# A two-layer hybrid diffusion block: merge units of mLSTM and GLA dealt out anew, GLA's scores issued a tile ahead

## The chip, the cores and the metric

The kernel runs on one core of a Trainium2 chip. The metric is the device time of one execution in microseconds. TensorE (PE) does matmuls and transposes, ScalarE (ACT) activations and copies out of PSUM, VectorE (DVE) elementwise work and scans, GpSimd (POOL) masks and indirect DMAs, SyncE (SP) streams the weights. Engines run their own instruction lists and meet at semaphores.

## The reference

Two layers over 256 context and 512 latent tokens, width 1024, float32. Each layer: adaLN-modulated norm, four token-mixer branches of width 256, their merge, and an expert-choice MoE with 16 experts. In layer 1 only the latent tokens are needed as queries. What matters here:

```
mLSTM (4 heads, 2 directions):  s = exp(d_log - m_t) * (q k^T);  h = (s v) / max(|den|, exp(-m_t))
GLA   (4 heads, 2 directions):  S_t = diag(exp(ge)) S + k^T v;   o = mask(q_dec k_inv^T) v + q_dec S0
merge:  g = sigmoid(h @ w_gate + b_gate);  p = y_branch @ w_branch
        y = sum over the four branches of g * p, then @ w_out
```

The merge of one branch needs only that branch's output y and the layer's input h. So the merge of branch n can be computed while branch n+1 is.

## The kernel before

Each engine has its own function per stage: `mla`, `mlstm`, `gla`, `diff`, `merge`, `moe`. The token axis is held as 6 tiles of 128 (2 context, 4 latent). TensorE writes to eight PSUM banks. They are dealt to three kinds of job by `ring`: "a" (ScalarE empties them), "d" (VectorE empties them) and "g" (merge units). A job that would take a bank still in use waits for its semaphore (`a_free`, `d_free`, `g_free`).

A **merge unit** is one 128 x 256 piece of a branch's gate and projection: 8 matmuls over h (line 539) and 2 over y (line 541) on TensorE, each shown as two in the profile since float32 takes two passes; a Tanh on ScalarE (`gates`); one or two operations on VectorE (`merged`). A branch has 24 units in layer 0 and 16 in layer 1. Those of the first branch run inside mLSTM, those of mLSTM inside GLA, and so on. How many run where is written out by hand and must be the same on all three engines: `ML_GAP` at the opening of mLSTM, `ml_quota` in its 24 steps, `ML_END` after them; `gl_quota` and `GL_END` for GLA. Before the change `ML_GAP` and `ML_END` are 3; the steps get 18 units in layer 0 and 10 in layer 1, spread evenly. GLA has 4, 1 and 1 per step (first direction) and 3, 2 and 1 per step (second) in layer 0; 4, 1, 1 per step and 1, 0, 1 per step in layer 1; then 2.

**mLSTM.** TensorE projects (lines 460, 467) and runs the opening units. VectorE scans the gates for two directions on 8 partitions and gives `ml_m`; ScalarE's Exp gives `ml_rows`, on which TensorE transposes (line 673). POOL carries rows through DRAM and back as a broadcast (`ml_bc0`). Then 4 heads of 6 steps: `products` (line 682, q k^T for key tile j), ScalarE's weights W(j) (waits for PV of step j-2, since `m_W` has two buffers), POOL's mask, VectorE's multiply (line 1482, gives `ml_s`), TensorE's PV (line 698). Products run a step ahead. At the end of a head VectorE normalises the sums (`x_free`) before it takes the next head's products.

**GLA.** After the projections and the alpha matmuls (line 729), ScalarE and VectorE form decays. Per direction: VectorE's scan gives `gl_g`, four Exps of ScalarE give `gl_e`, VectorE's operands give `gl_ops`; TensorE transposes (line 474), 11 chunk matmuls (line 741) feed VectorE's state recurrence (lines 1470 and 1482, `gl_state`); then per query tile scores (line 749), VectorE's mask into `g_A` (`gl_att`), and matmuls with the states and values (lines 758, 761). Units in GLA cycle through two banks, 6 and 7.

The weights stream through three ring slots of 2 MB each, in the order of `layer_pieces`.

Of the kernel before, what the change touches and what calls it, by code (L numbers as in the profile page):

```python
# [19 lines left out]
ALU = mybir.AluOpType  # L20
AF = mybir.ActivationFunctionType
AX = mybir.AxisListType
P = 128
# [4 lines left out]
T = CTX + LAT  # L28
NT = T // P
# [130 lines left out]
def hybrid_layers(nc, I, out, stop=None):  # L160
    ctx = ExitStack()
    with ctx:
# [104 lines left out]
        def ml_quota(L):  # L267

            n = branch_units(L) - ML_GAP - ML_END
            return [(s + 1) * n // (4 * NT) - s * n // (4 * NT) for s in range(4 * NT)]  # L270

# [5 lines left out]

        ML_GAP, ML_END, GL_END, DF_GAP, DF_END = 3, 3, 2, 2, 2

        def gl_quota(L):  # L280

            return (4, 1, 1, 3, 2, 1) if len(chunks(L)) == 3 else (4, 1, 1, 1, 0, 1)

# [66 lines left out]
        g_y = area(19 * T, NT * 256).rearrange("p (t c) -> p t c", t=NT)  # L350
        g_A = area(21 * T, 512)
        g_sl = area(21 * T + 512, 256)
# [79 lines left out]
        def _(pe):  # L432
# [218 lines left out]
            def mlstm(L):  # L651
# [33 lines left out]
                for h in range(4):  # L685

                    products(h, 0)
                    for j in range(NT):
                        if j + 1 < NT:
                            products(h, j + 1)  # L690
                        merge_units(L, quota[h * NT + j])
                        pe.wait_ge(sems["ml_s"], c.nth("ml_s"))
                        if j == 0 and h >= 1:
                            pe.wait_ge(sems["x_free"], c.nth("x_free"))
                        for d in range(2):
                            ts = ml_tiles(L, d, j)
                            for t in ts:
                                ins = pe.matmul(banks[6 + d][:, t * 65:t * 65 + 65], m_W[:, j % 2, d, t * P:(t + 1) * P],
                                                m_v[:, j, h, :], start=(j == 0 and t == ts[0]),
                                                stop=(j == ml_last(d, t)), skip_group_check=True)  # L700
                        ins.then_inc(sems["pv_done"], 1)
# [5 lines left out]
            def gla(L):  # L707
# [18 lines left out]
                for d in range(2):  # L726
                    for off, n in SEG:
                        b = job("a")
                        pe.matmul(b[:, 0:n], wa[0:16, d, :], g_a[0:16, d, off:off + n], start=True, stop=True).then_inc(sems["a_done"], 1)
                for d in range(2):  # L730

                    merge_units(L, quota[3 * d])
                    pe.wait_ge(sems["gl_ops"], c.nth("gl_ops"))
# [3 lines left out]
                    for i in range(11):  # L737
                        ch = gla_chunk(d, i)
                        t, r = ch // 2, (ch % 2) * 64
                        b = job("d")  # L740
                        pe.matmul(b[:, 0:256], g_ke[r:r + 64, t * P:(t + 1) * P], g_v[r:r + 64, t, :],
                                       start=True, stop=True).then_inc(sems["d_done"], 1)
                        if i % 4 == 3 and i // 4 < quota[3 * d + 1]:
                            merge_units(L, 1)
                    pe.wait_ge(sems["gl_state"], c.nth("gl_state"))
# [5 lines left out]

                    for t in QT:
                        scores(t)
                        merge_units(L, quota[3 * d + 2])
                        pe.wait_ge(sems["gl_att"], c.nth("gl_att"))
                        b = job("d")
                        for r in range(2):
                            pe.matmul(b[r * 64:r * 64 + 64, 0:256], g_qd[:, t * P + r * 64:t * P + r * 64 + 64],
                                      g_S[:, 2 * t + r, :], start=True, stop=False, skip_group_check=True)
                        for h in range(4):  # L760
                            ins = pe.matmul(b[:, h * 64:h * 64 + 64], g_A[:, h * P:(h + 1) * P],
                                            g_v[:, t, h * 64:h * 64 + 64], start=False, stop=True, skip_group_check=True)
                        ins.then_inc(sems["d_done"], 1)
                merge_units(L, GL_END)
                finish_transposes(g_y)

            def diff(L):
# [251 lines left out]
        def _(act):  # L1019
# [189 lines left out]
            def mlstm(L):  # L1209
# [19 lines left out]
                act.sem_inc(sems["ml_qk"], 1)  # L1229
                softplus_parts(m_F[0:8, 0, :], gF[0:8, :], "ml_x", "ml_l")  # L1230
                act.wait_ge(sems["ml_m"], c.nth("ml_m"))
                do(m_F[0:8, :, :], m_F[0:8, :, :], AF.Exp, scale=-1.0)
                act.sem_inc(sems["ml_rows"], 1)
                gates(L, ML_GAP)
                act.wait_ge(sems["ml_e"], c.nth("ml_e"))
# [18 lines left out]
            def gla(L):  # L1254
# [37 lines left out]
                for d in range(2):  # L1292
# [7 lines left out]
                    act.sem_inc(sems["gl_e"], 1)  # L1300
                    gates(L, quota[3 * d] - 2 * (d == 0) + quota[3 * d + 1] + quota[3 * d + 2] * len(QT))
                finish(L, GL_END)
# [158 lines left out]
        def _(dve):  # L1461
# [248 lines left out]
            def mlstm(L):  # L1710
# [20 lines left out]
                for d in range(2):  # L1731
# [14 lines left out]
                    for i, (m, g) in enumerate(zip(runs(M_), runs(g_))):  # L1746
                        scan(m, g, g, NEG_BIG if i == 0 else M_[:, 0:1], ALU.max, ALU.max)
                    tt(F_, F_, M_, ALU.add)
                dve.sem_inc(sems["ml_m"], 1)
                dve.wait_ge(sems["d_done"], c.nth("d_done"))  # L1750
# [3 lines left out]
                dve.sem_inc(sems["ml_e"], 1)  # L1754
                merged(L, ML_GAP)
                quota = ml_quota(L)
# [48 lines left out]
            def gla(L):  # L1805
# [10 lines left out]
                for d in range(2):  # L1816
# [11 lines left out]
                    dve.sem_inc(sems["gl_g"], 1)  # L1828
                    merged(L, quota[3 * d] - 2 * (d == 0))
                    dve.wait_ge(sems["gl_e"], c.nth("gl_e"))  # L1830
# [7 lines left out]
                    for off, n in SEG:  # L1838
                        dve.wait_ge(sems["d_done"], c.nth("d_done"))
                        b = bank()  # L1840
                        copy(g_ke[:, off:off + n], b[:, 0:n])
                        dve.sem_inc(sems["d_free"], 1)

                    heads = cc("heads").unsqueeze(2).to_broadcast([P, 4, 64])
                    S(dve.memset(g_S[:, gla_chunk(d, 0), :], 0.0))
                    for i in range(11):
# [5 lines left out]
                        stt(g_S[:, z, :], g_S[:, a, :], s_ge[:, d, a:a + 1], g_sl, ALU.mult, ALU.add)  # L1852
                        if i % 4 == 3 and i // 4 < quota[3 * d + 1]:
                            merged(L, 1)
                    dve.sem_inc(sems["gl_state"], 1)
                    mask = cc(("m_fwd", "m_bwd")[d]).unsqueeze(1).to_broadcast([P, 4, P])
                    for t in QT:
                        dve.wait_ge(sems["d_done"], c.nth("d_done"))
                        b = bank()
                        tt(g_A.rearrange("p (h c) -> p h c", h=4), b[:, :].rearrange("p (h c) -> p h c", h=4), mask, ALU.mult)  # L1860
                        dve.sem_inc(sems["d_free"], 1)
                        dve.sem_inc(sems["gl_att"], 1)
                        merged(L, quota[3 * d + 2])
                        dve.wait_ge(sems["d_done"], c.nth("d_done"))
# [516 lines left out]
```

## Time and profile before

| | |
|---|---|
| median of 3 runs | 4409.82 us (4408.23 to 4410.06) |
| the profiled execution | 4399.55 us, span 4397.8 us |
| TensorE busy | 3719.3 us, 85% of the span |
| VectorE, ScalarE, POOL busy | 1176.6, 769.2, 127.0 us |
| chain that ended last | TensorE 65%, DMA 16%, VectorE 11%, ScalarE 5%, issue 3% |
| mean granted TensorE clock | 0.898 of 2.4 GHz |

The chain is the work that ended last, followed backwards from the last instruction. Matmul ends are modelled by the profiler, so TensorE's busy time holds some waiting inside a stream of matmuls. In a row of a timeline, the number in brackets is the idle time of that engine just before, and the arrow names what ended it. A granted clock of 0.5 is 1.2 GHz and of 1.0 is 2.4 GHz; a stretch between has had both.

### The profile page before, as it was taken

The page shows a single profiled execution, that of the slowest core. Times are in us where ns is not written, and L with a number is a line of the kernel's source. Part 1 is how long each engine was busy: PE and PEld are TensorE (multiplying, and loading weights), DVE is VectorE, ACT ScalarE, POOL GpSimd, SP SyncE. Part 2 cuts the span into 40 slices and gives each one's busy share as a digit, 9 for nine tenths or more (in the row PEclk, how much of TensorE's full clock was granted, in tenths as well). Part 3 has the DMA queues.
Part 4 walks back from the last instruction along what each step waited for, and adds up shares of the span by engine and source line. Part 5 has one row for each costly group of instructions (what it writes and reads, how often), then busy time and mean ns, then how long its engine had stood idle before and what let it go on. Part 6 is the DMA issues. An engine that isn't in the chain of part 4 may idle for free.

```text
span 4397.8 us, 62885 instructions
## 1 busy us (share of the span) xinstructions
PE 3719.3 (85%) x25844; PEld 2526.8 (57%) x25844; DVE 1176.6 (27%) x2860; ACT 769.2 (17%) x1604; POOL 127.0 (3%) x184
## 2 busy tenths in 40 slices
PE   7699899898999689999998669898879967877776
PEld 4355675656777467777775345665557734444443
DVE  0332322434651311111111242323346230101111
ACT  2221322102221300000001322222122130010011
POOL 0000000000000000000000000000000000000000
PEclk9899899897989889999999779798879979999998
DMA  4272101001011179999999101110000219999998
GB/s 181 84 272 75 41 20 67 10 24 43 25 53 72 71 258 350 344 351 337 349 345 329 43 0 36 48 48 29 32 35 25 99 62 365 379 379 379 385 381 307
DMA packets 326559, 740.25 MB, mean 168 GB/s; under 512 B 7808, under 2 KB 79488, under 8 KB 326288
## 3 DMA queue, kind: packets, MB, share of 16 engines
q1 hardware_dynamic: 314800, 695.29, 43.4%
q0 software_dynamic: 11616, 43.05, 3.4%
q8 instruction: 90, 1.47, 0.1%
q14 instruction: 53, 0.43, 0.0%
HBM read 713.09 MB, written 25.21 MB: 168 GB/s over the span
## 4 chain that ended last, share of the span: by engine, by line
PE 65%; DMA 16%; DVE 11%; ACT 5%; issue 3%; DVEq 0%; ACTq 0%; SPq 0%; POOL 0%; POOLq 0%
PE bank L539 11%; PE bank L947 8%; PE bank L467 7%; PE bank L920 7%; PE bank L460 5%; DMA ring<-in_w_e_up 5%; DMA ring<-in_w_e_gate 4%; PE bank L911 4%; PE bank L820 3%; DMA ring<-in_w_e_down 3%; DMA f_rows<-work,idx 3%; PE bank L629 3%; DVE work L1470 3%; ACT work L1024 3%; PE bank L541 2%
## 5 line engine op out<-in xcount | busy, mean ns | idle before, releaser
L539 PE MATMUL bank<-HT,ring 128*128 128x256 f32 x2560 | 641.3, 408 | 18.3 <-DVEq L1535 12.6
L539 PEld LDWEIGHTS bank<-HT,ring 128*128 128x128 f32 x2560 | 521.3, 207 | 134.1 <-issue 38.8
L947 PE MATMUL bank<-ring,work 128*96 128x512 f32 (+1 forms) x1408 | 471.1, 603 | 28.6 <-DMA ring<-in_w_e_down 27.2
L911 PE MATMUL bank<-ring,work 128*64 128x256 f32 x1536 | 384.4, 408 | 127.8 <-DMA ring<-in_w_e_up 68.8
L920 PE MATMUL bank<-work,ring 128*64 128x96 f32 x11264 | 480.8, 249 | 3.9 <-DVEq L1996 3.0
L920 PEld LDWEIGHTS bank<-work,ring 128*64 128x64 f32 x11264 | 474.3, 139 | 16.8 <-issue 15.2
L911 PEld LDWEIGHTS bank<-ring,work 128*64 128x64 f32 x1536 | 218.2, 147 | 268.0 <-DMA ring<-in_w_e_up 87.5
L912 PE MATMUL bank<-ring,work 128*64 128x256 f32 (+1 forms) x1536 | 368.9, 379 | 0.0
L947 PEld LDWEIGHTS bank<-ring,work 128*96 128x96 f32 (+1 forms) x1408 | 167.5, 151 | 296.0 <-issue 262.9
L1024 ACT ACTIVATE work<-bank,small 128x512 f32<-128x512 f32 (+3 forms) x248 | 144.6, 583 | 960.9 <-PE bank L947 497.0
L467 PE MATMUL bank<-ring,HT 128*128 128x512 f32 (+2 forms) x960 | 309.8, 487 | 0.0
L1027 ACT ACTIVATE work<-bank 128x256 f32<-128x256 f32 (+9 forms) x275 | 126.0, 458 | 818.3 <-PE bank L467 266.9
L467 PEld LDWEIGHTS bank<-ring,HT 128*128 128x128 f32 x960 | 178.4, 206 | 128.7 <-issue 121.9
L460 PE MATMUL bank<-HT,ring 128*128 128x512 f32 (+5 forms) x624 | 220.3, 515 | 9.7 <-ACTq L1092 6.2
L474 PE MATMUL bank<-const,work 128*128 128x128 f32 (+1 forms) x700 | 123.8, 324 | 91.4 <-DVEq L1837 29.6
L912 PEld LDWEIGHTS bank<-ring,work 128*64 128x64 f32 x1536 | 199.9, 146 | 2.0
L1024 ACT ACTIVATE YT<-bank,pack 128x256 f32<-128x256 f32 x160 | 75.7, 473 | 659.7 <-PE bank L541 641.9
L1024 ACT ACTIVATE X<-bank 128x384 f32<-128x384 f32 (+3 forms) x112 | 43.3, 386 | 784.7 <-PE bank L920 447.9
L460 PEld LDWEIGHTS bank<-HT,ring 128*128 128x128 f32 (+2 forms) x624 | 111.7, 181 | 116.6 <-issue 96.0
L1474 DVE TENSOR_SCALAR work<-bank,small 128x64 f32<-128x64 f32 (+2 forms) x72 | 35.4, 492 | 494.3 <-PE bank L947 439.1
L629 PEld LDWEIGHTS bank<-work 128*128 128x128 f32 x832 | 122.6, 229 | 74.9 <-DVEq L1623 44.8
L541 PE MATMUL bank<-YT 128*128 128x256 f32 x640 | 164.2, 379 | 0.0
(180 smaller groups left out, 3458.4 us busy)
## 6 DMA issues: line engine op xcount, KB each, us to landing
ring<-in_w_e_gate SPq DMA_DIRECT2D x64, 2048.0 KB, 10.4
ring<-in_w_e_up SPq DMA_DIRECT2D x64, 2048.0 KB, 13.4
ring<-in_w_e_down SPq DMA_DIRECT2D x64, 2048.0 KB, 9.6
ring<-in_w_ada SPq DMA_DIRECT2D x24, 2048.0 KB, 7.9
ring<-in_w_e_gate SPq DMA_DIRECT2D x32, 1536.0 KB
ring<-in_w_e_up SPq DMA_DIRECT2D x32, 1536.0 KB, 7.1
ring<-in_w_e_down SPq DMA_DIRECT2D x32, 1536.0 KB, 9.9
ring<-in_w_gate SPq DMA_DIRECT2D x16, 2048.0 KB, 8.5
```

The lines of the kernel that those rows point to most:

```text
L460: ins = pe.matmul(b[0:M, 0:n], w[:, k, c0:c0 + M], HT[:, k, off:off + n], start=(k == 0), stop=(k == KD - 1))
L467: ins = pe.matmul(b[:, 0:n], HT[:, k, t * P:(t + 1) * P], w[:, k, c0:c0 + n], start=(k == 0), stop=(k == KD - 1))
L539: pe.matmul(b[:, 0:256], w[:, k, d4 * P:(d4 + 1) * P], HT[:, k, off:off + 256], start=(k == 0), stop=(k == KD - 1))
L541: ins = pe.matmul(b[:, 256:512], wbr[:, m % 2, i, d4 * P:(d4 + 1) * P], YT[:, n_ % 2, i, off:off + 256], start=(i == 0), stop=(i == 1))
L629: ins = pe.matmul(b[:, 0:64], PT[:, t * P:(t + 1) * P], v[:, t, it[0], :], start=(t == 0), stop=(t == len(keys) - 1))
L820: ins = pe.matmul(b[:, :], mT[:, k, t * P:(t + 1) * P], w[:, k, :], start=(k == 0), stop=(k == KD - 1))
L911: pe.matmul(b[0:64, 0:256], e_xs[:, k, 0:64], w[:, k, 0:256], start=(k == 0), stop=(k == KD - 1))
L912: ins = pe.matmul(b[64:128, 0:n - 256], e_xs[:, k, 0:64], w[:, k, 256:n], start=(k == 0), stop=(k == KD - 1))
L920: ins = pe.matmul(b[lo:lo + 64, f * cap:(f + 1) * cap], w[:, k, c0:c0 + 64], e_xs[:, k, 0:cap], start=(k == 0), stop=(k == KD - 1))
L947: ins = pe.matmul(banks[6 + half][lo:lo + cap, :], e_hidT[:, at, 0:cap], w[:, k, half * 512:half * 512 + 512], start=(f == 0), stop=(f == ...
L1024: c.seq(act.activation(*a, **kw))
L1470: S(dve.tensor_tensor(o_, a, b, op))
```

## The change

In mLSTM five units run at the opening (three before), of which VectorE merges two between its two scan directions. The steps get four units per head in layer 0 (steps 0, 1, 3, 4) and two in layer 1 (steps 0 and 3). In step 0 the unit is issued ahead of the second products, not behind them. In GLA more units run at the start of a direction and fewer in the steps; VectorE merges them behind the copies of the transposed keys, not ahead of its operands; the units cycle through five banks, for which TensorE first waits until ScalarE has emptied all "a" banks; the scores of tile i+1 are issued and masked before tile i's output, with two buffers for `g_A`, the second in `g_t1`, which is free by then. The numbers of units per branch stay.

```diff
         def ml_quota(L):
-            n = branch_units(L) - ML_GAP - ML_END
-            return [(s + 1) * n // (4 * NT) - s * n // (4 * NT) for s in range(4 * NT)]
+            m = (branch_units(L) - ML_GAP - ML_END) // 4
+            head = [sum(j == k * NT // m for k in range(m)) for j in range(NT)]
+            return head * 4
-        ML_GAP, ML_END, GL_END, DF_GAP, DF_END = 3, 3, 2, 2, 2
+        ML_GAP, ML_EARLY, ML_END, GL_END, DF_GAP, DF_END = 5, 2, 3, 2, 2, 2
         def gl_quota(L):
-            return (4, 1, 1, 3, 2, 1) if len(chunks(L)) == 3 else (4, 1, 1, 1, 0, 1)
+            q = [(6, 2, (1, 0, 1, 0, 1, 1)), (4, 2, (1, 0, 1, 0, 1, 1))] if len(chunks(L)) == 3 else \
+                [(5, 1, (1, 0, 1, 0)), (3, 1, (1, 0, 1, 0))]
+            return q
-        g_A = area(21 * T, 512)
+        g_A = (area(21 * T, 512), g_t1[:, 0:512])
...
 TensorE, mlstm
                     products(h, 0)
                     for j in range(NT):
+                        if j == 0:
+                            merge_units(L, quota[h * NT])
                         if j + 1 < NT:
                             products(h, j + 1)
-                        merge_units(L, quota[h * NT + j])
+                        if j > 0:
+                            merge_units(L, quota[h * NT + j])
 TensorE, gla
+                all_free("a")
+                ring("g", (6, 7, 0, 1, 2))
                 for d in range(2):
-                    merge_units(L, quota[3 * d])
+                    at_start, at_states, at_step = quota[d]
+                    merge_units(L, at_start)
...
-                        if i % 4 == 3 and i // 4 < quota[3 * d + 1]:
-                            merge_units(L, 1)
+                        if i == 5:
+                            merge_units(L, at_states // 2)
+                    merge_units(L, at_states - at_states // 2)
...
-                    for t in QT:
-                        scores(t)
-                        merge_units(L, quota[3 * d + 2])
+                    scores(QT[0])
+                    for i, t in enumerate(QT):
+                        if i + 1 < len(QT):
+                            scores(QT[i + 1])
+                        merge_units(L, at_step[i])
                         pe.wait_ge(sems["gl_att"], c.nth("gl_att"))
...
                 finish_transposes(g_y)
+                ring("g", (6, 7))
 ScalarE, mlstm
                 softplus_parts(m_F[0:8, 0, :], gF[0:8, :], "ml_x", "ml_l")
+                gates(L, ML_EARLY)
                 act.wait_ge(sems["ml_m"], c.nth("ml_m"))
                 do(m_F[0:8, :, :], m_F[0:8, :, :], AF.Exp, scale=-1.0)
                 act.sem_inc(sems["ml_rows"], 1)
-                gates(L, ML_GAP)
+                gates(L, ML_GAP - ML_EARLY)
 VectorE, mlstm
                     tt(F_, F_, M_, ALU.add)
+                    if d == 0:
+                        merged(L, ML_EARLY)
                 dve.sem_inc(sems["ml_m"], 1)
 VectorE, gla
                     dve.sem_inc(sems["gl_g"], 1)
-                    merged(L, quota[3 * d] - 2 * (d == 0))
                     dve.wait_ge(sems["gl_e"], c.nth("gl_e"))
...
                         copy(g_ke[:, off:off + n], b[:, 0:n])
                         dve.sem_inc(sems["d_free"], 1)
+                    merged(L, at_start - 2 * (d == 0))
...
-                        if i % 4 == 3 and i // 4 < quota[3 * d + 1]:
-                            merged(L, 1)
+                        if i == 7:
+                            merged(L, at_states // 2)
                     dve.sem_inc(sems["gl_state"], 1)
+                    merged(L, at_states - at_states // 2)
...
+                    masked(0)
+                    for i, t in enumerate(QT):
+                        if i + 1 < len(QT):
+                            masked(i + 1)
+                        merged(L, at_step[i])
                         dve.wait_ge(sems["d_done"], c.nth("d_done"))
```

`masked(i)` waits for the scores, multiplies the bank by the mask into `g_A[i % 2]`, and gives `d_free` and `gl_att`.

## Rows read from the trace of the kernel before

**Rows 1.** Windows: length, busy time by engine, granted clock, DMA share; four stretches.
```profile
448.60:668.40 219.80, 193.38 (x904) 153.87 (x904) 74.77 (x153) 59.11 (x88) 17.39 (x54) 0.87 0.09 30
747.90:948.00 200.10, 164.99 (x705) 125.04 (x704) 84.28 (x157) 32.20 (x48) 0.00 (x0) 0.86 0.04 15
2738.20:2918.80 180.60, 156.62 (x681) 121.14 (x682) 62.57 (x130) 51.16 (x76) 12.54 (x38) 0.80 0.11 37
2984.00:3142.00 158.00, 125.09 (x495) 90.86 (x494) 69.04 (x132) 29.82 (x42) 0.00 (x0) 0.82 0.06 20
```

**Rows 2.** Timeline (start, us, what), TensorE, opening of mLSTM, layer 0.
```profile
453.05 3.62 PE L539 MATMUL bank<-HT,ring 128*128 128x256 f32 x16
...
457.37 3.62 PE L539 MATMUL bank<-HT,ring 128*128 128x256 f32 x16
...
473.09 2.73 PE L673 MATMUL bank<-const,work 8*128 8x8 f32 x24 [11.24 <-ACTq L1233]
...
484.54 1.22 PE L682 MATMUL bank<-work 64*128 64x256 f32 x2 [4.16 <-DVEq L1773]
485.69 4.95 PE L698 MATMUL bank<-work 128*128 128x65 f32 x22
...
498.26 2.56 PE L698 MATMUL bank<-work 128*128 128x65 f32 x22
```

**Rows 3.** Timeline, VectorE: last scan work of each direction, layer 0.
```profile
464.47 0.94 DVE L1470 TENSOR_TENSOR work<-work 8x768 f32<-8x768 f32 x1
...
470.47 0.95 DVE L1470 TENSOR_TENSOR work<-work 8x768 f32<-8x768 f32 x1
```

**Rows 4.** Timeline, ScalarE: first weights of mLSTM, layer 0.
```profile
479.15 4.04 ACT L1024 ACTIVATE work<-work 128x768 f32<-128x768 f32 x5 [1.64 <-DMA work<-m_rows]
```

**Rows 5.** Timeline, TensorE, from head 0 to head 1, layer 0.
```profile
520.60 1.23 PE L698 MATMUL bank<-work 128*128 128x65 f32 x10
...
527.82 1.22 PE L682 MATMUL bank<-work 64*128 64x256 f32 x2 [3.66 <-DVEq L1773]
528.97 5.55 PE L539 MATMUL bank<-HT,ring 128*128 128x256 f32 x16
```

**Rows 6.** Timelines, ScalarE and VectorE: the work for step 5 of head 0.
```profile
514.12 1.16 ACT L1024 ACTIVATE work<-work 128x128 f32<-128x128 f32 x2 [0.59 <-PE bank L698]
...
516.20 1.02 DVE L1482 SCALAR_TENSOR_TENSOR work<-bank,work 128x128 f32<-128x128 f32 x2 [2.17 <-POOLq L2164]
```

**Rows 7.** Timeline, TensorE, mLSTM of layer 1: steps and a head boundary.
```profile
2790.95 1.23 PE L698 MATMUL bank<-work 128*128 128x65 f32 x10
...
2807.09 3.68 PE L698 MATMUL bank<-work 128*128 128x65 f32 x16 [2.94 <-DVEq L1774]
...
2818.85 1.90 PE L698 MATMUL bank<-work 128*128 128x65 f32 x16
2820.67 1.12 PE L682 MATMUL bank<-work 64*128 64x512 f32 x2
```

**Rows 8.** Timeline, TensorE, GLA of layer 0.
```profile
764.72 5.44 PE L539 MATMUL bank<-HT,ring 128*128 128x256 f32 x16 [6.31 <-DVEq L1535]
...
782.43 1.54 PE L474 MATMUL bank<-const,work 128*128 128x128 f32 x6 [7.09 <-DVEq L1837]
...
811.93 0.65 PE L758 MATMUL bank<-work 128*64 128x256 f32 x4
...
867.97 1.54 PE L474 MATMUL bank<-const,work 128*128 128x128 f32 x6 [7.09 <-DVEq L1837]
```

**Rows 9.** Timelines, ScalarE's Exps, VectorE's operands and one state chunk, layer 0.
```profile
769.88 2.60 ACT L1024 ACTIVATE work<-work 128x768 f32<-128x768 f32 x3 [7.66 <-DVEq L1828]
...
777.03 1.95 DVE L1470 TENSOR_TENSOR work<-work 128x768 f32<-128x768 f32 x2
...
787.39 0.42 DVE L1470 TENSOR_TENSOR work<-bank,const 128x256 f32<-128x256 f32 x1
```

**Rows 10.** Timeline, TensorE, second direction of GLA, layer 1.
```profile
3086.49 1.54 PE L474 MATMUL bank<-const,work 128*128 128x128 f32 x6 [9.14 <-DVEq L1837]
```

More of the change, by code:

```diff
@@ L267, in ml_quota @@
         def ml_quota(L):
-            n = branch_units(L) - ML_GAP - ML_END
-            return [(s + 1) * n // (4 * NT) - s * n // (4 * NT) for s in range(4 * NT)]
+            m = (branch_units(L) - ML_GAP - ML_END) // 4
+            assert 4 * m + ML_GAP + ML_END == branch_units(L)
+            head = [sum(j == k * NT // m for k in range(m)) for j in range(NT)]
+            return head * 4
         MG_ROWS = 6
@@ L276, in xn_first @@
             return 1 + sum(len(qtiles(l)) + NT for l in range(L))
-        ML_GAP, ML_END, GL_END, DF_GAP, DF_END = 3, 3, 2, 2, 2
+        ML_GAP, ML_EARLY, ML_END, GL_END, DF_GAP, DF_END = 5, 2, 3, 2, 2, 2
         def gl_quota(L):
-            return (4, 1, 1, 3, 2, 1) if len(chunks(L)) == 3 else (4, 1, 1, 1, 0, 1)
+            q = [(6, 2, (1, 0, 1, 0, 1, 1)), (4, 2, (1, 0, 1, 0, 1, 1))] if len(chunks(L)) == 3 else \
+                [(5, 1, (1, 0, 1, 0)), (3, 1, (1, 0, 1, 0))]
+            assert sum(a + b + sum(x) for a, b, x in q) + GL_END == branch_units(L)
+            return q
         def item_units(L, i):
@@ L760, in gla @@
                         for h in range(4):
-                            ins = pe.matmul(b[:, h * 64:h * 64 + 64], g_A[:, h * P:(h + 1) * P],
+                            ins = pe.matmul(b[:, h * 64:h * 64 + 64], g_A[i % 2][:, h * P:(h + 1) * P],
                                             g_v[:, t, h * 64:h * 64 + 64], start=False, stop=True, skip_group_check=True)
@@ L1300, in gla @@
                     act.sem_inc(sems["gl_e"], 1)
-                    gates(L, quota[3 * d] - 2 * (d == 0) + quota[3 * d + 1] + quota[3 * d + 2] * len(QT))
+                    at_start, at_states, at_step = quota[d]
+                    gates(L, at_start - 2 * (d == 0) + at_states + sum(at_step))
                 finish(L, GL_END)
@@ L1754, in mlstm @@
                 dve.sem_inc(sems["ml_e"], 1)
-                merged(L, ML_GAP)
+                merged(L, ML_GAP - ML_EARLY)
                 quota = ml_quota(L)
@@ L1828, in gla @@
                     dve.sem_inc(sems["gl_g"], 1)
-                    merged(L, quota[3 * d] - 2 * (d == 0))
+                    at_start, at_states, at_step = quota[d]
                     dve.wait_ge(sems["gl_e"], c.nth("gl_e"))
@@ L1852, in gla, with masked @@
                         stt(g_S[:, z, :], g_S[:, a, :], s_ge[:, d, a:a + 1], g_sl, ALU.mult, ALU.add)
-                        if i % 4 == 3 and i // 4 < quota[3 * d + 1]:
-                            merged(L, 1)
+                        if i == 7:
+                            merged(L, at_states // 2)
                     dve.sem_inc(sems["gl_state"], 1)
+                    merged(L, at_states - at_states // 2)
                     mask = cc(("m_fwd", "m_bwd")[d]).unsqueeze(1).to_broadcast([P, 4, P])
-                    for t in QT:
+                    def masked(i):
                         dve.wait_ge(sems["d_done"], c.nth("d_done"))
                         b = bank()
-                        tt(g_A.rearrange("p (h c) -> p h c", h=4), b[:, :].rearrange("p (h c) -> p h c", h=4), mask, ALU.mult)
+                        tt(g_A[i % 2].rearrange("p (h c) -> p h c", h=4), b[:, :].rearrange("p (h c) -> p h c", h=4), mask, ALU.mult)
                         dve.sem_inc(sems["d_free"], 1)
                         dve.sem_inc(sems["gl_att"], 1)
-                        merged(L, quota[3 * d + 2])
+                    masked(0)
[3 more added lines that the diff above has]
+                        merged(L, at_step[i])
                         dve.wait_ge(sems["d_done"], c.nth("d_done"))
```

## Prediction

> **What bounds the kernel now.** I read the chain of waits in order of time first: over half the span it is TensorE's own work, and the units of the merge (the matmuls of lines 539 and 541) stand in it all through mLSTM and GLA of both layers. So time is only to be had where TensorE idles or runs at the low clock. Then I cut those four stretches out by windows [rows 1]: 758.5 us together, TensorE busy 640.1, so 118.4 idle. Their granted clocks (0.87, 0.86, 0.80, 0.82) mean that about a third of the time, 246 us, was at 1.2 GHz; with the idle part taken off, at most 128 us of work ran at half speed and cost at most 64 us. No rearranging here can give more than 118 + 64 = 182 us. Last I read TensorE's timeline in each stretch, to see which wait ends each gap, and beside it ScalarE's and VectorE's, to see what the releaser itself waits for. The reader is to see that the gaps lie in few places (openings, head boundaries, GLA's states) and none inside the steps.
>
> Terms: a merge unit takes 4.32 us at 2.4 GHz (start to start) [rows 2]. PV of a step is 2.56 us for 11 tiles, 1.23 for 5 [rows 2, 5], 1.90 for 8; a product of 512 columns 1.12 [rows 7], at a pace of 1.07 in a row of them, one of 256 columns about 0.6. Units are only dealt out anew: 24 in layer 0, 16 in layer 1, before and after. What counts is what lies in a gap and what is late next.
>
> **mLSTM, layer 0, opening.** Three units end at 461.7; TensorE idles 11.24 us, then 4.16 us, and its work between is at half speed (first PV 4.95 us for what later takes 2.56) [rows 2]. The gaps end by VectorE's scans, whose last row ends at 471.4 [rows 3], then a copy through DRAM to the broadcast, which ScalarE gets at 479.15 [rows 4], then mask and product. After the change two more units and one behind the first products stand there. VectorE merges two units between its directions, behind the row that ends at 465.41 [rows 3]: about 0.5 us each (0.42 for an operation on 256 columns [rows 9] and the handing over), so ml_m and all behind it come 1.05 us later. That is also when the bank of unit 4 comes free (three banks): TensorE idles 461.7 to 466.05, is cold after it (unit 4 at 6.2 us, between the 4.32 at full speed and 8.6 at half), unit 5 ends at 476.6, 2.5 us after ml_rows. Transposes 1.4, products 2.0, unit 4.3, next products 2.2, PV 0 at 486.5 (old 485.69); PV 0 2.56, product 1.1, unit 4.3: PV 1 starts at 494.4 against 498.26 [rows 2], with 3 more units done (13.0 us). The ScalarE and VectorE work for step 1 is ready by then. Rest of head 0: one unit fewer, minus 4.3. So head 0 ends 3.9 + 4.3 = 8.2 us earlier.
>
> **Head boundaries, layer 0.** The last PV ends at 521.83; TensorE makes three products and waits 3.66 us for VectorE, which normalises the head; product and unit behind it run partly at half speed (1.22 for 256 columns, unit 5.55 where 3.6 is usual) [rows 5]: about 6 us per boundary. With a unit ahead of the second products TensorE gets to them at t0 + 2.0 + 4.3 + 1.1 = t0 + 7.4; VectorE is ready at t0 + 6.0 (527.82 less 521.83). No gap, and no fall of the clock. A head is then pure work: products 2 x 1.7 + 4 x 1.07 = 7.7, PV 2 x 2.56 + 4 x 1.23 = 10.0, four units 17.3, together 34.9. Heads 1 to 3 took 45, 43.5 and 45 us with 5, 4, 5 units: 28.8 less. Layer 0: 8.2 + 28.8 = **37.0 us**.
>
> **Are the steps without a unit covered?** The price of an empty step is the chain from PV(j-2) to PV(j): ScalarE's weights from 514.12 on, POOL's mask, VectorE's two passes to 517.22 [rows 6], 3.3 us with the handing over. TensorE has PV(j-1) and two products in that time. In layer 0 the empty steps are 2 and 5, with units at 1 and 4 inside each such span: covered, 0 us. In layer 1 they are 1, 2, 4, 5. Step 2: 1.12 + 1.90 + 1.12 = 4.1 against 3.8 for wider tiles: covered. Step 5: 1.12 + 1.23 = 2.35 against 3.3: 1 us late, four times.
>
> **mLSTM, layer 1.** The opening has the same shape. Units to 2751.3, gap to 2755.9, units 4 and 5 to 2766.4, PV 0 at 2774.2 and PV 2 at 2780.2 where it was 2790.95 [rows 7], with two more units done. Rest of head 0: one unit as before and 1 us late, minus 1.0. The boundaries idled 2.94 us and ran the next 8-tile PV at 3.68 instead of 1.90 [rows 7]. New head: products 6.4, PV 2 x 1.90 + 4 x 1.23 = 8.6, two units 8.6, 1.0 late: 24.7 against 35.2, 33.6 and 34.9, so 29.6 less. Layer 1: 10.7 - 1.0 + 29.6 = **39.3 us**.
>
> **GLA, layer 0.** (a) TensorE now waits until ScalarE has emptied the four alpha banks: 1.2 us, an estimate between 0 and the 2.9 us of four such copies. (b) Five banks: it no longer stops behind two units (6.31 us) [rows 8], and six run without a stop to about 776.7. (c) gl_e is given at 772.7, but VectorE starts the operands only at 777.03 [rows 9], behind two merges; now at once, so the transposes start at 778.2 and not at 782.43 [rows 8], with 2 more units done: 4.2 + 8.6 = 12.8. (d) The merges come back between the copies and the state recurrence: four at 1.03 us, 4.1 us on VectorE's chain, under which TensorE has three small matmuls only. Eleven chunks at 1.10 us [rows 9] follow, a unit at chunk 5 and one at the end, partly at half speed (6.6 and 5 us). First PV at 809.5, old 811.93 [rows 8], with 9 units done, old 6: 2.4 + 13.0 = 15.4. (e) The last five steps cost 6.84 us with a unit and 2.5 without, and hide VectorE's 2.5 us; a tile ahead and two g_A buffers leave nothing to wait for. Second direction: in the old order its 3rd unit ended at 860.9 and held VectorE's merges and operands, transposes at 867.97 [rows 8]. Now the operands are ready 12.7 us after the last PV, under four units (17.3): transposes 3 us earlier with one unit more, 7.3. States and first PV about the old length for the same three units, 0.6 less. Layer 0: 15.4 + 7.9 = **23.3 us**, the tail of the branch unchanged (VectorE's norm).
>
> **GLA, layer 1.** First direction: transposes 4.8 us earlier, one more unit (9.1); the states lose 3.1 us to three merges, gain 4 where the chunks were held by a unit: 10. Second direction: the gap of 9.14 us before the transposes [rows 10] held one unit; three fit, and they start 0.7 us earlier: 9.3; three merges ahead of the states and a cold unit at their end cost 1.8. Together **17.5 us**.
>
> **Sum.** 37.0 + 39.3 + 23.3 + 17.5 = 117.1 us. From this I take 7 us for low clock after the gaps that stay (two of 4.4 us in the openings, four of 3 to 4 us ahead of the states), on which I put only part of the doubling: 110. The profiled execution took 4399.55 us around a span of 4397.8, so 4289.5; the median of the runs is 4409.82, 10.3 above it, so **4300 us**. DMA: the pieces for GLA and differential attention are asked for as before and needed over 60 us later; I cost it at nothing. Without this cover the 2 MB pieces are late by what GLA has become shorter at most, some 20 us per layer.
>
> **A rule on the clock.** The rows show half speed behind the gaps of 11.24, 4.16, 3.66 and 2.94 us [rows 2, 5, 7], and the high level in steps of small matmuls without a gap (1.90 for 8 tiles [rows 7]). The Trainium skill ("TensorE: Matmul & The Clock Gate", section "A second HAM failure mode: psum-queue depth-cycling") says that short idles between groups of matmuls that cycle through PSUM banks can be enough to let the clock swing between its levels. By that rule, steps thinned to small groups could run at half speed; it is rival 2 below.
>
> **Rivals.**
> 1. The empty steps are not covered: only one step is in flight, and each of 24 (8 in layer 0, 16 in layer 1) is 2.2 us late (3.3 + 1.2 against 2.3 of work). 53 us of the gain go: 4353. For it: the cover in layer 1 is 0.3 us thick. Against: TensorE goes from PV to PV in the old empty steps with no gap [rows 7].
> 2. The clock falls in the thinned steps. Layer 1: products and PV of four heads doubled, 4 x 15.0 = 60; layer 0: two empty steps per head, 4 x 2 x 2.3 = 18. Gain 32: 4378. For it: layer 1 has the lowest clock [rows 1]. Against: the low stretches there start at gaps.
> 3. Slower. The chain of ScalarE, POOL and VectorE paces the heads, not TensorE. Then a unit ahead of the second products holds VectorE's pass of step 1 at eight heads, 8 x 4.3 = 34, GLA's 14 merges lie on the states at 1.03 us each, 14, the early merges and bank waits add 2.1 + 2.4, and nothing comes back from thinner steps: 4463. It decides from 117 / 24 = 4.9 us lateness per empty step; the rows allow 1.
> 4. The change moves units from covered steps to places equally covered: 4410. Against: the openings' 11 us gaps have no matmul in them [rows 2].
>
> **Chances.** Forecast 0.74, rival 1 0.12, rival 2 0.07, rival 3 0.04, rival 4 0.03. The forecast's own range is 4282 to 4325 (low: no clock loss and no late step 5, some boundary work warmer; high: cold units throughout the gaps' wake). To leave out under 0.2 the range goes to rival 1 and a little more slack below: 4278 to 4353. A measurement tells 0.2% (9 us) from no change. Faster: forecast and rivals 1, 2: 0.93; same 0.03; slower 0.04.
>
> **What would show it.** TensorE: the 11.24 us gap is about 4.4, the four waits of products on VectorE are gone, and none of the 9.14, 7.09 and 6.31 us gaps of GLA is over 5. mLSTM at 183 and 141 us (from 219.8 and 180.6), GLA about 177 and 141 (from 200.1 and 158). GLA's new gaps are 3 to 4 us after the third chunk. Granted clock over 0.9 in mLSTM. Wrong would be: gaps ahead of PV in steps 2 and 5 of over 1 us (rival 1), PV of 5 tiles at 2.4 us there (rival 2), heads over 45 us (rival 3).

## The result, and the profile after

| | before | after |
|---|---|---|
| median | 4409.94 us (4 runs, 4408.23 to 4416.89) | 4306.62 us (4 runs, 4302.52 to 4313.83) |
| ratio after / before | | 0.9765, 95% interval 0.9748 to 0.9782 |
| span of the profiled execution | 4397.8 us | 4300.8 us |

103.3 us less were measured, 110 forecast.

The same four stretches by windows, as in [rows 1] (length, busy PE, PEld, DVE, ACT, POOL, granted clock, DMA share, GB/s):

```profile
450.60:633.60 183.00, 178.65 (x905) 143.20 (x905) 75.11 (x154) 59.10 (x88) 18.07 (x54) 0.98 0.11 36
713.90:886.00 172.10, 157.50 (x705) 120.40 (x705) 84.31 (x158) 31.28 (x46) 0.00 (x0) 0.92 0.05 15
2682.70:2839.80 157.10, 149.14 (x680) 114.04 (x681) 62.55 (x130) 51.15 (x76) 12.54 (x38) 0.89 0.12 42
2908.30:3040.50 132.20, 119.44 (x489) 88.20 (x489) 69.15 (x132) 27.50 (x38) 0.00 (x0) 0.86 0.05 16
```

Together 644.4 us with 39.7 idle; before 758.5 with 118.4. Of the 114.1 us less, 78.7 are idle time and 35.4 are busy time: but for a few, the same matmuls (2779 and 2785 records), under a higher granted clock (0.98, 0.92, 0.89 and 0.86, where it was 0.87, 0.86, 0.80 and 0.82). Since the window of GLA starts at its first unit, which now waits for banks, I measure GLA below from the alpha matmuls to the first matmul of differential attention:

| | mLSTM 0 | GLA 0 | mLSTM 1 | GLA 1 | sum |
|---|---|---|---|---|---|
| before | 220.0 | 206.4 | 180.6 | 159.8 | 766.8 |
| after | 183.0 | 179.4 | 157.2 | 137.7 | 657.3 |
| less | 37.0 | 27.0 | 23.4 | 22.1 | 109.5 |
| forecast | 37.0 | 23.3 | 39.3 | 17.5 | 117.1 |

TensorE's timeline at the opening of mLSTM, layer 0, answers to [rows 2]:

```profile
459.32 3.62 PE L544 MATMUL bank<-HT,ring 128*128 128x256 f32 x16
...
467.93 6.65 PE L544 MATMUL bank<-HT,ring 128*128 128x256 f32 x16 [4.13 <-DVEq L1552]
...
482.75 3.72 PE L544 MATMUL bank<-HT,ring 128*128 128x256 f32 x16
...
488.60 0.70 PE L687 MATMUL bank<-work 64*128 64x256 f32 x2 [0.21 <-DVEq L1792]
489.23 2.67 PE L706 MATMUL bank<-work 128*128 128x65 f32 x22
...
497.30 2.56 PE L706 MATMUL bank<-work 128*128 128x65 f32 x22
```

The gap of 11.24 us is one of 4.13; the one of 4.16 is 0.21, with a unit ahead of it; the first PV takes 2.67 us, not 4.95. PV 1 starts 46.7 us after the first unit (450.58), where it was 49.6, with three more units done: 2.9 us less, where 3.9 was forecast. The head boundary, which answers to [rows 5]:

```profile
514.21 2.34 PE L706 MATMUL bank<-work 128*128 128x65 f32 x20
516.48 1.55 PE L687 MATMUL bank<-work 64*128 64x512 f32 x4
517.96 3.72 PE L544 MATMUL bank<-HT,ring 128*128 128x256 f32 x16
...
522.48 1.55 PE L687 MATMUL bank<-work 64*128 64x512 f32 x4
523.96 2.67 PE L706 MATMUL bank<-work 128*128 128x65 f32 x22
```

No row has a bracket: PV of steps 4 and 5, products, unit, products, PV, without a gap. A head is 34.7 us (514.21 to 548.94). In layer 1 (answers to [rows 7]) step 5 waits, and what follows is slow:

```profile
2734.97 1.33 PE L706 MATMUL bank<-work 128*128 128x65 f32 x10
2737.34 2.39 PE L706 MATMUL bank<-work 128*128 128x65 f32 x10 [1.03 <-DVEq L1793]
2739.66 2.07 PE L687 MATMUL bank<-work 64*128 64x512 f32 x2
2741.66 6.42 PE L544 MATMUL bank<-HT,ring 128*128 128x256 f32 x16
...
2795.60 1.33 PE L706 MATMUL bank<-work 128*128 128x65 f32 x10 [1.03 <-DVEq L1793]
2796.86 1.12 PE L687 MATMUL bank<-work 64*128 64x512 f32 x2
2797.91 5.41 PE L544 MATMUL bank<-HT,ring 128*128 128x256 f32 x16
```

The wait is the 1.0 us forecast. That the next PV (2.39 for 1.33), product (2.07 for 1.12) and unit (6.42 for 3.72) ran at half speed or near it was not in the sum. The wait is the same in all four heads, what follows is not: in the third head (last three rows) PV and product ran at full speed and only the unit was slow. From the wait's end to the end of the unit the four heads lose about 4.8, 3.4, 1.8 and 3.3 us against full speed.

GLA of layer 0, TensorE, answers to [rows 8] (a row with x6 at line 752 is three chunks):

```profile
743.12 0.88 PE L479 MATMUL bank<-const,work 128*128 128x128 f32 x6 [0.21 <-DVEq L1856]
745.19 1.13 PE L752 MATMUL bank<-work 64*128 64x256 f32 x6 [1.19 <-DVEq L1861]
750.26 3.42 PE L752 MATMUL bank<-work 64*128 64x256 f32 x6 [3.94 <-DVEq L1871]
753.61 5.48 PE L544 MATMUL bank<-HT,ring 128*128 128x256 f32 x16
...
767.36 1.88 PE L761 MATMUL bank<-work 128*128 128x512 f32 x4
```

The transposes wait 0.21 us and not 7.09. Before the fourth chunk is the new gap of 3.94 us, in which VectorE merges; behind it chunks and unit are partly at half speed.

### The profile page after: what moved, and what is told of

Same layout as the page of the kernel before. It is cut to its first block, busy times and chain, and to the rows that moved or that the text cites. A ratio compares the mean times of both kernels' runs of the same rounds, so it can differ in the third digit from the quotient of the medians.

```text
span 4300.8 us, 62883 instructions
## 1 busy us (share of the span) xinstructions
PE 3689.4 (86%) x25844; PEld 2503.2 (58%) x25844; DVE 1177.2 (27%) x2860; ACT 769.2 (18%) x1604; POOL 127.7 (3%) x184
## 4 chain that ended last, share of the span: by engine, by line
PE 66%; DMA 16%; DVE 10%; ACT 5%; issue 3%; DVEq 0%; ACTq 0%; SPq 0%; POOL 0%; POOLq 0%
PE bank L544 11%; PE bank L962 9%; PE bank L472 7%; PE bank L935 7%; PE bank L465 5%; DMA ring<-in_w_e_up 5%; PE bank L926 4%; DMA ring<-in_w_e_gate 4%; PE bank L835 3%; DMA f_rows<-work,idx 3%; PE bank L634 3%; ACT work L1039 3%; DMA ring<-in_w_e_down 3%; PE bank L546 2%; DVE work L1487 2%
## 5 line engine op out<-in xcount | busy, mean ns | idle before, releaser
L544 PE MATMUL bank<-HT,ring 128*128 128x256 f32 x2560 | 637.9, 406 | 15.9 <-DVEq L1552 7.8
L472 PEld LDWEIGHTS bank<-ring,HT 128*128 128x128 f32 x960 | 179.3, 207 | 129.5 <-issue 121.9
L1491 DVE TENSOR_SCALAR work<-bank,small 128x64 f32<-128x64 f32 (+2 forms) x72 | 35.4, 492 | 494.5 <-PE bank L962 442.0
```

Source lines behind the costliest of these rows:

```text
L472: ins = pe.matmul(b[:, 0:n], HT[:, k, t * P:(t + 1) * P], w[:, k, c0:c0 + n], start=(k == 0), stop=(k == KD - 1))
L544: pe.matmul(b[:, 0:256], w[:, k, d4 * P:(d4 + 1) * P], HT[:, k, off:off + 256], start=(k == 0), stop=(k == KD - 1))
```

## The experiments

Stage lengths repeat closely from profile to profile (mLSTM 0: 183.0 to 183.1 in all that have its new form; GLA within 2 us, mostly 0.6), so one profile tells a stage. Only mLSTM 1 spreads more: 155.7 to 160.4 in the six profiles that have the changed kernel's code for it, 177.5 to 181.1 in the four with the old. The total of one run tells less than a stage: the stretch from the output projection of layer 0 to mLSTM 1, which no change here touches, took 1337.6 to 1364.1 us in the fourteen profiles.

**The two halves alone.** `ml_alone`: the diff's lines in `mlstm`, `ml_quota` and `ML_GAP`. `gla_alone`: the rest.

> Only mLSTM's part of the change; GLA as before. Theory (each gap is filled where it lies, the parts add up): mLSTM 183 us in layer 0 and 157 us in layer 1 as in the changed kernel, GLA 200 and 158 as before, time lower than before by 60 us, about 4350. Rival (part of the gain is a loan: what is taken from one stage is given back by the next, through banks or weights that come late): the stretches before differential attention end less early than 37 + 23 us, and the two halves together are over 10 us off the whole change's 103 us.

> Only GLA's part of the change; mLSTM as before. Theory (the parts add up): mLSTM 219.8 and 180.6 us as before, from the alpha matmuls to differential attention 179.6 us in layer 0 (206.4 before) and 137.7 in layer 1 (159.8 before), time lower than before by 49 us, about 4361. Rival (a loan between stages): the sum of the two halves misses the whole by over 10 us.

`ml_alone`: 4354.16 us, ratio 0.9879 (0.985 to 0.9908); mLSTM 183.0 and 157.3, GLA 206.5 and 159.7. `gla_alone`: 4362.5 us, ratio 0.991 (0.9878 to 0.9942); mLSTM 220.6 and 177.5, GLA 179.3 and 137.9. Each stage has its new length where its own part is there and, but for 3 us in mLSTM 1, its old one elsewhere: they add, nothing is lent. The medians of that chip (before 4402.09) give 48 + 40 = 88 us, 16 less than the whole. That is over the 10 us which the rival named as its mark. The intervals (13 and 14 us to either side) allow it, though, and the stages, which add to 109, show no loss between them.

**The unit of step 0 behind the second products.**

```diff
-                        if j == 0:
-                            merge_units(L, quota[h * NT])
                         if j + 1 < NT:
                             products(h, j + 1)
-                        if j > 0:
-                            merge_units(L, quota[h * NT + j])
+                        merge_units(L, quota[h * NT + j])
```

> The changed kernel with the unit of step 0 behind the second products, as before. Theory (the unit is worth its place ahead of the products only where the third products wait for VectorE): layer 0 has the three waits of 3.65 us back, with low clock behind each, and one in the opening, mLSTM 183 -> 199 to 206 us; in layer 1, where a step has one product and not two and three banks reach, nothing changes, 157 us. Rival (the number of units per step alone makes the gain): 183 and 157. Second rival (VectorE's norm at the head boundary holds both layers alike): both longer by about 18 us.

One run, 4338.85 us. mLSTM 208.9 us in layer 0, 157.5 in layer 1: the theory, with the loss at 25.9 us a little over its range. TensorE, head boundary in layer 0:

```profile
523.98 2.41 PE L687 MATMUL bank<-work 64*128 64x512 f32 x6
530.11 1.22 PE L687 MATMUL bank<-work 64*128 64x256 f32 x2 [3.72 <-DVEq L1789]
531.26 5.92 PE L544 MATMUL bank<-HT,ring 128*128 128x256 f32 x16
```

The gap of [rows 5] is back. The same units in the same steps are worth 26 us less in another place, since in layer 0 the products of steps 0 and 1 need four banks (two a step) and their ring has three, so that the last waits until VectorE gives `d_free` (line 1789). In layer 1 they need two, and the place is worth nothing.

**The opening as before**, `ML_GAP, ML_EARLY, ML_END` = 3, 0, 5.

> The changed kernel with three units at the opening of mLSTM, none merged early, and the two others behind the steps. Theory: the two units cost their full 8.6 us at the end, the opening's low clock comes back (3 to 5 us), ml_m comes 1 us earlier: mLSTM longer by 10 to 13 us in each layer, 195 and 169. Rival (the opening is bound by the chain of scans, Exp and broadcast, so what TensorE does in it is worth nothing, and the early merges only delay it): shorter by 1 us, or longer by the 8.6 us alone.

One run, 4311.47 us. mLSTM 191.3 and 163.6: 8.2 and 6.4 us longer, under the 10 to 13 of the theory and near the rival's units alone; by the spread of mLSTM 1 the second is anything from 3 to 8. The time, 5 us over the changed kernel's median, is one run and does not show it. TensorE at the opening of layer 0:

```profile
473.17 2.73 PE L678 MATMUL bank<-const,work 8*128 8x8 f32 x24 [11.24 <-ACTq L1249]
475.82 2.92 PE L687 MATMUL bank<-work 64*128 64x512 f32 x4
478.68 5.48 PE L544 MATMUL bank<-HT,ring 128*128 128x256 f32 x16
...
486.44 2.67 PE L706 MATMUL bank<-work 128*128 128x65 f32 x22
```

The gap of 11.24 us is back, but the slow work behind it lies in the time in which TensorE would wait for the broadcast anyway. PV 0 starts 37.7 us after the first unit, 38.7 with the early units. So they bring their 8.6 us less about the 1 us by which they delay VectorE. What is left of the opening's gain, some 8 us, goes by subtraction to the unit of step 0 and the clock at PV 0.

**Layer 1's second unit at step 4.**

```diff
-            head = [sum(j == k * NT // m for k in range(m)) for j in range(NT)]
+            head = [1, 1, 0, 1, 1, 0] if m == 4 else [1, 0, 0, 0, 1, 0]
```

> The changed kernel, layer 1 with its second unit of a head at step 4 and not at step 3. Theory (the 1.03 us that PV waits at step 5 costs over four times its length, because TensorE runs the PV, the products and the unit behind it at half speed): with the unit behind PV of step 3 the wait is covered, 4 x 1.03 us and 4 x about 3.2 us of half speed go, mLSTM of layer 1 157.2 -> 140 us, as the prediction had it. Rival (step 3, now empty, is late in its place: 3.5 us of work against a chain of 3.5 to 3.8): 150 to 158 us. Second rival (thin steps run at half speed whether or not there is a gap): 155 to 158 us.

4288.36 us, ratio 0.9742 (0.9713 to 0.977). mLSTM of layer 1 is 139.5 us. Its window, and TensorE through steps 2 to 5:

```profile
2682.60:2822.10 139.50, 135.57 (x680) 104.84 (x681) 62.57 (x130) 51.17 (x76) 12.54 (x38) 0.98 0.14 48
```

```profile
2728.39 1.33 PE L706 MATMUL bank<-work 128*128 128x65 f32 x10
2729.65 1.12 PE L687 MATMUL bank<-work 64*128 64x512 f32 x2
2730.71 3.72 PE L544 MATMUL bank<-HT,ring 128*128 128x256 f32 x16
...
2735.13 2.34 PE L706 MATMUL bank<-work 128*128 128x65 f32 x20
2737.40 1.12 PE L687 MATMUL bank<-work 64*128 64x512 f32 x2
2738.45 3.72 PE L544 MATMUL bank<-HT,ring 128*128 128x256 f32 x16
```

Step 3 is not late, no unit of the steps behind head 0's first runs slowly, and the clock is 0.98. Four waits of 1.03 us had cost 17.7, of which 4.1 are the waits and the rest slow work. As thin steps as before run at full speed, so the second rival falls, and with it the forecast's rival 2. One slow unit stays, in both kernels and with no wait of 0.2 us or more ahead of it:

```profile
2712.82 5.41 PE L544 MATMUL bank<-HT,ring 128*128 128x256 f32 x16
```

The ratio's interval overlaps the changed kernel's; that this place is worth 17.7 us is shown by the stage.

**GLA's first unit of the states behind chunk 2.**

```diff
-                        if i == 5:
-                            merge_units(L, at_states // 2)
-                    merge_units(L, at_states - at_states // 2)
+                        if i == 2:
+                            merge_units(L, 1)
+                    merge_units(L, at_states - 1)
```

VectorE merges one behind chunk 7 and `at_states - 1` behind the last.

> The changed kernel with the first unit of GLA's states behind chunk 2, where TensorE waits 3.9 us while VectorE merges, and not behind chunk 5 (in layer 1, where one unit follows the chunks, that one). Theory (the merges ahead of the recurrence are free where a unit fills TensorE's wait): layer 0 179.4 -> 171 us, layer 1 137.7 -> 129 us. Rival (VectorE's recurrence is the bound of this phase, and a unit anywhere before its end only delays the next chunk by as much as it saves): within 2 us of 179.4 and 137.7.

4301.77 us, ratio 0.9754 (0.9732 to 0.9776). GLA 175.5 and 138.8: half of the theory in layer 0, nothing in layer 1. The gaps of 3.9 us are filled, but waits for `gl_state` come instead. In layer 1 (us in total, times, longest):

```profile
PE bank L761 <- DVEq L1875: 7.4, 2, 3.7
```

VectorE's recurrence sets the end of the phase there, as the rival has it. In the time the run can't be told from the changed kernel.

**VectorE's merges ahead of the Exps' wait**: `merged(L, at_start - 2 * (d == 0))` moved back before `dve.wait_ge(sems["gl_e"], ...)`.

> The changed kernel with VectorE's merges of GLA's opening units ahead of the wait for the Exps, as before. Theory (placing them later only moves them: operands 5.5 and 6.4 us later in layer 0, but 4.1 us of merging go from the states in each direction; 1.9 and 5.5 against 3.1 in layer 1): 183 us in layer 0 and 139 in layer 1, so the gain is that more units run there, not that the merges moved. Rival (the earlier operands are the gain, as the prediction's term of 4.2 us per direction has it, and the states do not feel the merges): longer by 8 to 12 us in layer 0 and 5 to 8 in layer 1.

One run, 4325.73 us. GLA 187.0 and 144.0, 7.6 and 6.2 us longer: the rival, or just under it. TensorE in layer 0:

```profile
750.31 1.54 PE L479 MATMUL bank<-const,work 128*128 128x128 f32 x6 [7.09 <-DVEq L1857]
752.83 5.29 PE L752 MATMUL bank<-work 64*128 64x256 f32 x12 [0.98 <-DVEq L1862]
```

The gap of 7.09 us of [rows 8] is back in both directions; from transposes to scores it is 21.1 us and not 24.2. So the states give 3.1 us back where I expected 4.1, and the transposes come some 7 us later in each direction of layer 0 where I expected 5.5 and 6.4: the last merge can't begin before the last unit has ended, and VectorE's operands stand behind it.

**GLA's scores in their own step**: `scores(t)` and `masked(i)` each at its own turn, the two `g_A` buffers kept.

> The changed kernel with GLA's scores in their own step, not a tile ahead. Theory (with no unit in a step TensorE waits for VectorE's mask of 0.69 us and the handing over, 1.1 to 1.3 us, in 4 steps of each layer, and the low clock behind it can double that): layer 0 179.4 -> 184 to 188 us, layer 1 137.7 -> 142 to 146 us. Rival (the matmuls with the states, which need no mask, or the next tile's work cover it): no change within 1 us.

One run, 4317.99 us. GLA 182.5 and 141.3, 3.1 and 3.6 us longer, under the theory's range: four waits in a layer,

```profile
778.95 0.65 PE L770 MATMUL bank<-work 128*64 128x256 f32 x4 [0.94 <-DVEq L1882]
779.53 1.10 PE L773 MATMUL bank<-work 128*128 128x64 f32 x8
```

and the matmuls behind them at full speed. The tile ahead is worth about its waits.

**Merges behind the recurrence**, with layer 1's unit at step 4.

```diff
-                    merged(L, at_start - 2 * (d == 0))
...
-                        if i == 7:
-                            merged(L, at_states // 2)
+                        if i in (2, 6):
+                            merged(L, 1)
                     dve.sem_inc(sems["gl_state"], 1)
-                    merged(L, at_states - at_states // 2)
+                    merged(L, at_start - 2 * (d == 0) + at_states - 2)
```

On TensorE, one unit behind chunk 2 and `at_states - 1` behind chunk 6.

> The changed kernel with layer 1's second unit at step 4, and in GLA VectorE's merges of the opening units behind the state recurrence, one merge and one unit behind chunk 2 and behind chunk 6 (in layer 1 no unit behind chunk 6). Theory (the states' phase is VectorE's: copies, merges, eleven chunks; the merges cost their 3 to 4 us there as long as they stand ahead of it, and the units are free if they are issued where TensorE waits): from transposes to scores 24.2 -> 17.7 us in layer 0, 21.4 and 22 -> 16.4 in layer 1; from the alpha matmuls to differential attention 179.4 -> 166 us and 137.7 -> 127 us; mLSTM of layer 1 140; the time about 40 us under the changed kernel, 4266. Rival (VectorE pays the same merges ahead of the masks, where TensorE then waits): GLA within 3 us of the changed kernel, time about 4288.

4286.43 us, ratio 0.9731 (0.9715 to 0.9748). GLA 174.2 and 138.6. The phase is 19.4 us in layer 0 (of the 17.7 expected), but it ends in a wait, and the scores run at half speed (3.78 for 1.88). In layer 1 the phases are 22.0 and 18.2 us where 16.4 was expected, and GLA gains nothing. In layer 0:

```profile
761.76 3.78 PE L760 MATMUL bank<-work 128*128 128x512 f32 x4 [3.21 <-DVEq L1873]
765.33 4.31 PE L544 MATMUL bank<-HT,ring 128*128 128x256 f32 x16
```

The theory failed for the time: 20 of its 40 us came, 17.7 of them from step 4. It is the fastest kernel, but not distinguishable from `step4`.

**The changed kernel and the kernel before again.**

> The changed kernel once more, word for word, to see what of the difference between runs lies in stages that nothing touched. Theory: mLSTM 183.0, GLA 179.4 and 137.7 us within 0.6 us, mLSTM of layer 1 157.2 within 2; the stretch of MoE 0 and latent attention 1, which has been 1337 to 1364 us in nine profiles, anywhere in that range. Rival (the change slows that stretch by 7 us, 1337.6 to 1344.3, as the two profiles say): 1344 within 1 us.

> The kernel before once more, word for word. The changed kernel's span fell by 97 us where its four changed stages fell by 109: the rest lies mostly in MoE 0 and latent attention 1 (1337.6 us in the profile before, 1340 to 1364 in eleven profiles of other kernels). Theory (that stretch varies from one execution to the next, through the expert weights' DMA and the clock, and the profile before was a lucky one): 1342 to 1360 us here. Rival (the change lengthens it): 1337.6 within 1.5 us. mLSTM and GLA 220, 180.6, 206.4 and 159.8 us, the two of layer 1 within 3 us, for the low clock behind their gaps.

> The kernel before a third time, word for word, for the same question: theory, 1342 to 1360 us from the output projection of layer 0 to mLSTM of layer 1; rival, 1337.6 within 1.5 us.

`changed_again`: 4305.4 us, ratio 0.9771 (0.9753 to 0.9789); mLSTM 183.0 and 160.4 (3 us over, outside the 2 expected), GLA 179.4 and 138.2; the stretch from the output projection of layer 0 to mLSTM 1 is 1344.1. That alone would fit the rival. The kernel before took 4408.39 and 4406.67 us, one run each; its mLSTM and GLA are again within 0.7 us of the first profile, and the stretch is 1344.4 and 1347.2, against 1337.6. So the change need not lengthen it; the profile that the forecast rests on had a short one.

## Why the prediction was right

**Bound and places.** Right: TensorE's gaps at openings, boundaries and states were the whole matter; halves and single parts each moved their own stage, and others by about 3 us at most. One step on the way is wrong: "at most 128 us of work ran at half speed" takes all idle time to lie at 1.2 GHz. Windows on the gaps show otherwise, 0.62 in the one of 11.24 us and 0.73 in the one of 6.31, so 128 is the least and not the most, and 182 us is no upper bound. Nothing else in the sum uses it.

**mLSTM, layer 0: 37.0 forecast, 37.0 measured.** The mechanism was right (`unit_behind`: the place of the unit is the cause), the equality to a tenth is luck: head 0 ended 7.2 us earlier and not 8.2, the rest gave 29.8 and not 28.8. Of the opening `opening_back` gives about 8 us to the two early units. The gap left was 4.13 us for 4.35.

**Cover of the empty steps: right in time, wrong in price.** Every step was as covered as worked out, and step 5 of layer 1 was late by 1.03 us for 1.0. The mis-sized term is mLSTM of layer 1, 39.3 forecast, 23.4 measured: I counted the wait at its length, 4 us in four heads, and it cost 17.7, since each was followed by slow work. `step4` removes the waits and gives 139.5 us, within 2 us of what I had forecast for the stage with them. Of the 15.9 us by which the stage missed its forecast 13.7 are this; the other 2.2 lie elsewhere, 1.4 of them in the opening, where the unit of step 0 took 5.41 us for 3.72. The signs that were to show me wrong came here: a gap of over 1 us ahead of PV in step 5, a PV of 5 tiles at 2.4 us behind it, and a granted clock of 0.89 and not over 0.9.

**GLA: 40.8 forecast, 49.1 measured.** The shape was right: the first PV of layer 0 came 63.5 us behind the alpha matmuls, 64.4 forecast. The excess grows step by step, 1 to 2 us at each of the states' phases, where I had put the units behind the chunks at 5 to 7 us and some of them ran at full speed (3.72 us and the two short matmuls of line 546). In the first direction of layer 0 that is 0.9 us; what makes up the rest of the excess is not separated. `merges_first` shows that the operands ahead of the merges are a gain of their own, 7.6 and 6.2 us, where (c) and (d) had nearly set the one against the other. The step part (e) is right: without the tile ahead, 0.94 us per empty step.

**The 7 us taken off for the clock** were put on the openings' gaps and those ahead of the states, not on step 5, where the loss came. That the four stages still add to 109.5 us, with 117.1 less 7 forecast, is luck: two errors of 16 and 8 us in opposite directions left 8, and the 7 happened to cover them.

**DMA at nothing.** Right: no gap for a weight piece in these stages. The span shows less than the stages, 97 against 109.5, in stretches that the change does not touch: 6.7 us from the output projection of layer 0 to mLSTM 1 (1337.6 us in one profile, 1344.4 and 1347.2 in two others of the same kernel), 2.0 ahead of mLSTM 0 and 4.0 behind GLA 1. The last was 1254.4 to 1255.6 us in three profiles of the kernel before and 1258.7 and 1259.3 in two of the changed one, but 1254.0 in `chunk2`; whether it is chance stays open.

**Rivals.** 1 is out (steps 2 and 3 are covered, even empty). 2 is out as stated (`step4`), though its slow work appears behind the wait of step 5. By the rule of the Trainium skill's page "TensorE: Matmul & The Clock Gate" ("A second HAM failure mode: psum-queue depth-cycling"), frequent short idles between groups of matmuls let the clock swing: this case's traces agree for the 1.03 us waits of layer 1, and not for the 0.94 us waits in `scores_in_step`, behind which everything ran at full speed. 3 and 4 are out.

## What to carry to other kernels

Where side work fills a main engine's gaps, list for each gap what its releaser waits for; a piece of side work is worth most ahead of the instruction that would wait, and one place in the queue was worth 26 us here. Keep one piece inside each span of the longest dependency chain rather than at even distances: 1 us of lateness cost over 4. When the phase is bound by the other engine's recurrence, filling the main engine's gaps stops paying.

## What the runs showed of the hardware

A wait of 1.03 us between small matmuls (65 columns) was followed by slow work in each of four heads, though in one of them only in the unit (5.41 us for 3.72), with PV and product ahead of it at full speed. Waits of 0.94 us behind a product of 512 columns were not (granted clock 1.00 from 775 to 790 us in `scores_in_step`), nor was the wait of 1.19 us ahead of GLA's first chunks (1.00 there, 745.19 to 746.30 us in the changed kernel), though only 1.1 us of work stood between it and the next wait. And in the opening of layer 1 the clock was 1.00 up to 2712.8 us and 0.67 over the unit behind it, without an idle time of 0.2 us between. So the length of a gap alone does not tell whether the clock falls; what does is not shown, since no run changes one thing and holds the rest. In `late_merges` a gap of 3.21 us slowed the scores to 3.78 us and the unit behind only to 4.31. The cost of the clock is not the same from run to run either: the same mLSTM of layer 1 took 155.7, 155.7, 157.2, 157.3, 157.3 and 160.4 us in six profiles of kernels that have the same code for it; in the one of 160.4 PV behind the wait was slow in all four heads, in the other five in three.
